# Memory values of a two-layer decoder step: the value slabs become the moving operand

## The reference

```python
def mem_kv(mem, w_kv):
    B, M, _ = mem.shape                     # 1, 256, 1024
    k, v = jnp.split(jnp.einsum('bmd,de->bme', mem, w_kv), 2, axis=-1)
    return k.reshape(B, M, M_HEADS, M_HD), v.reshape(B, M, M_HEADS, M_HD)
...
s = jnp.einsum('bthd,bmhd->bhtm', q, mk) * M_SCALE
o = jnp.einsum('bhtm,bmhd->bthd', softmax(s), mv)
```

## Time and profile before

| what | value |
|---|---|
| median of 3 runs | 2196.74 us (2196.38 to 2198.42) |
| profiled execution, its own time | 2196.69 us |
| its span, first to last instruction | 2194.9 us |
| PE busy in the span | 2154.5 us, 98% |
| PE weight loads | 1961.4 us, 89% |
| DVE, ACT, POOL busy | 77%, 60%, 46% |
| memory products, layer 0 and layer 1 | 69 to 161 us, 1156 to 1236 us |

### The profile page before, as it was taken

How to read it: one execution, slowest core, us unless ns; L and a number is a source line. 1 busy time by engine, 2 the same in 40 slices (tenths; PEclk the granted TensorE clock), 3 DMA queues, 4 the chain that set the end, 5 groups by cost and what they waited for, 6 DMA issues and landing times.

```text
span 2194.9 us, 45729 instructions
## 1 busy us (share of the span) xinstructions
PE 2154.5 (98%) x15517; PEld 1961.4 (89%) x15517; DVE 1686.1 (77%) x3908; ACT 1316.4 (60%) x3002; POOL 1014.2 (46%) x820
## 2 busy tenths in 40 slices
PE   8989999999999999999999999999999999999998
PEld 8879799999999877888888988999999998788887
DVE  7766489979999856666656656999799996566666
ACT  6544474557777555555566645645777765555555
POOL 6764447997777610000043344589877774000000
PEclk9999999999999999999999999999999999999999
DMA  7548554554444665555545584455444447555554
GB/s 263 161 143 326 206 179 156 171 176 156 155 159 156 206 218 182 193 194 194 193 164 180 191 362 136 166 168 171 167 155 160 156 147 246 195 192 193 194 195 135
DMA packets 112422, 409.32 MB, mean 186 GB/s; under 512 B 16553, under 2 KB 18769, under 8 KB 107089
## 3 DMA queue, kind: packets, MB, share of 16 engines
q1 hardware_dynamic: 107744, 391.45, 52.2%
q0 software_dynamic: 4528, 15.86, 2.3%
HBM read 397.11 MB, written 10.14 MB: 186 GB/s over the span
## 4 chain that ended last, share of the span: by engine, by line
PE 62%; DVE 16%; POOL 7%; issue 4%; ACT 2%; POOLq 0%; ACTq 0%; DVEq 0%
PE banks L2712 10%; PE banks L2714 10%; PE banks L2713 10%; POOL slab_ring_lo L2150 7%; DVE one_hot_gates L2458 7%; PE banks L2201 5%; PE banks L2202 5%; PE banks L2203 5%; PE banks L296 3%; PE banks L297 3%; PE banks L298 3%; DVE slab_ring_lo L272 2%; DVE expert_activations L2475 2%; PE banks L2223 1%; DVE expert_activations L2466 1%
## 5 line engine op out<-in xcount | busy, mean ns | idle before, releaser
L2150 POOL TENSOR_TENSOR slab_ring_lo<-slab_ring,u_hi 128x512 fp32r<-128x512 f32 x504 | 663.1, 1340 | 167.5 <-ACT u_hi L2255 166.7
L2201 PE MATMUL banks<-operand_hi,u_hi 128*128 128x264 f32 x2016 | 584.8, 290 | 1.6 <-POOL slab_ring_lo L2150 1.6
L2203 PE MATMUL banks<-operand_hi,slab_ring_lo 128*128 128x264 f32 x2048 | 583.3, 285 | 0.0
L2202 PE MATMUL banks<-operand_lo,u_hi 128*128 128x264 f32 x2016 | 573.5, 284 | 0.0
L272 POOL TENSOR_TENSOR slab_ring_lo<-slab_ring,slab_hi 128x512 fp32r<-128x512 f32 x162 | 216.5, 1341 | 593.7 <-ACT slab_hi L262 593.0
L2656 DVE TENSOR_TENSOR v_lo<-slab_ring,v_hi 128x512 fp32r<-128x512 f32 x508 | 350.0, 691 | 117.7 <-ACT v_hi L2616 113.0
L2712 PE MATMUL banks<-v_hi,w_hi 128*128 128x512 f32 x1000 | 391.1, 391 | 3.4 <-DVE w_lo L2652 2.2
L2714 PE MATMUL banks<-v_lo,w_hi 128*128 128x512 f32 x1000 | 389.2, 389 | 0.0
L2713 PE MATMUL banks<-v_hi,w_lo 128*128 128x512 f32 x1000 | 389.2, 389 | 0.0
L2255 ACT ACTIVATE u_hi<-slab_ring 128x512 fp32r<-128x512 f32 x504 | 317.7, 631 | 117.8 <-PE banks L2203 115.2
L2203 PEld LDWEIGHTS banks<-operand_hi,slab_ring_lo 128*128 128x128 f32 x2048 | 385.4, 188 | 0.0
(11 more groups left out here) (443 smaller groups left out, 3794.1 us busy)
## 6 DMA issues: line engine op xcount, KB each, us to landing
slab_ring<-in_u SPq DMA_DIRECT2D x256, 512.0 KB
slab_ring<-in_v SPq DMA_DIRECT2D x256, 512.0 KB
slab_ring<-in_proj SPq DMA_DIRECT2D x144, 512.0 KB
cache_k_T<-in_cache_k SPq DMA_DIRECT2D x16, 1024.0 KB, 8.7
cache_v<-in_cache_v SPq DMA_DIRECT2D x16, 1024.0 KB, 11.8
memory_T<-in_mem POOLq DMA_DIRECT2D x2, 1024.0 KB, 6.5
sample_state<-in_state POOLq DMA_DIRECT2D x8, 256.0 KB, 3.9
out_mem_k_out<-mem_k_T SPq DMA_DIRECT2D x16, 128.0 KB, 3.0
```

Source lines behind the costliest of these rows:

```text
L2150: nc.gpsimd.tensor_tensor(step.ring_lo[:, s, g * HC:(g + 1) * HC, :], step.slab(s)[:, g * HC:(g + 1) * HC, :], part[:, buf].bitcast(F32), ...
L2201: nc.tensor.matmul(bank, part[:, buf, k, :], xh[:, c, :], start=(c == 0), stop=False)
L2202: nc.tensor.matmul(bank, part[:, buf, k, :], xl[:, c, :], start=False, stop=False)
L2203: last = nc.tensor.matmul(bank, step.ring_lo[:, s, c, :], xh[:, c, :], start=False, stop=(c == DC - 1))
```

## The change

For the value slabs the roles are exchanged. The memory tokens become stationary, as two blocks of 128 tokens per chunk, and the slab's 128 columns move. The result comes out with tokens on the partitions, in two halves of 128 columns of one bank, so the two transposes, the copy to `memory_values_T`, that buffer and two semaphores go. A value slab has 8 chunks x 2 token blocks x 3 = 48 matmuls with 128 moving columns in place of 24 with 256, and one ScalarE copy in place of two, issued right behind the product. Keys are made as before.

```diff
     def product(self, pe, k):
         if k >= 2:
             pe.wait_ge(self.read, k - 1)
-        product(self.step, pe, self.base + k, self.bank_of + k % 2, None, self.mem, NMEM)
-
-    def transpose(self, pe, k):
         if k < DC:
-            return
-        nc = self.step.nc
-        pe.wait_ge(self.copied, k - DC + 1)
-        for m in range(NMEM // P):
-            last = nc.tensor.transpose(self.bank(k)[:, NMEM + m * P:NMEM + (m + 1) * P],
-                                       self.values_T[:, k % 2, m * P:(m + 1) * P], self.step.ident)
-        last.then_inc(self.turned, 1)
+            product(self.step, pe, self.base + k, self.bank_of + k % 2, None, self.mem, NMEM)
+        else:
+            self.values(pe, k)
+
+    def values(self, pe, k):
+        step, nc, n = self.step, self.step.nc, self.base + k
+        j = step.split_number[n]
+        xh, xl = self.mem
+        wh, wl = step.slab_hi[:, (j + 1) % 2], step.ring_lo[:, n % SLOTS]
+        for c in range(DC):
+            if c % HC == 0:
+                pe.wait_ge(step.slab_lo_ready[c // HC], j + 1)
+            for m in range(NMEM // P):
+                out, ts = self.bank(k)[:, m * P:(m + 1) * P], slice(m * P, (m + 1) * P)
+                nc.tensor.matmul(out, xh[:, c, ts], wh[:, c, :], start=(c == 0 and m == 0), stop=False)
+                nc.tensor.matmul(out, xl[:, c, ts], wh[:, c, :], start=False, stop=False)
+                last = nc.tensor.matmul(out, xh[:, c, ts], wl[:, c, :], start=False,
+                                        stop=(c == DC - 1 and m == NMEM // P - 1))
+            if c == HC - 1:
+                last.then_inc(step.half_product_done, 1)
+        last.then_inc(step.product_done, 1)
 
     def copy(self, act, k):
         step, nc = self.step, self.step.nc
         act.wait_ge(step.product_done, step.product_count(self.base + k))
-        if k < DC:
-            nc.scalar.activation(step.mem_k[:, k, :], self.bank(k)[:, 0:NMEM], ACT.Copy).then_inc(self.read, 1)
-        else:
-            nc.scalar.activation(self.values_T[:, k % 2, :], self.bank(k)[:, 0:NMEM], ACT.Copy).then_inc(self.copied, 1)
-
-    def copy_transposed(self, act, k):
-        if k < DC:
-            return
-        step, nc = self.step, self.step.nc
-        act.wait_ge(self.turned, k - DC + 1)
-        out = step.mem_v[:, :, (k - DC) * P:(k - DC + 1) * P]
-        nc.scalar.activation(out, self.bank(k)[:, NMEM:2 * NMEM].rearrange("p (m f) -> p m f", m=NMEM // P),
-                             ACT.Copy).then_inc(self.read, 1)
+        out, bank = step.mem_k[:, k % DC, :], self.bank(k)[:, 0:NMEM]
+        if k >= DC:
+            out = step.mem_v[:, :, (k - DC) * P:(k - DC + 1) * P]
+            bank = bank.rearrange("p (m f) -> p m f", m=NMEM // P)
+        nc.scalar.activation(out, bank, ACT.Copy).then_inc(self.read, 1)
...
                 def memory_pair(k):
                     memory.product(pe, k)
-                    memory.transpose(pe, k - 1)
...
                     memory.copy(act, k)
-                    memory.copy_transposed(act, k - 1)
```

More of the change, by code:

```diff
@@ L898, in __init__ @@
         self.step, self.base, self.mem, self.bank_of = step, base, mem, bank
-        self.values_T = None
         self.read = step.sem(f"memory_chunk_copied{layer}")
-        self.copied = step.sem(f"memory_value_chunk_copied{layer}")
-        self.turned = step.sem(f"memory_value_chunk_transposed{layer}")
     def bank(self, k):
@@ L969, in hgrn_pool_mixer @@
         mem_hi = sb("memory_hi", [P, DC, NMEM], ctx, F32R)
-        values_T = sb("memory_values_T", [P, 2, NMEM])
         rows = sb("sample_value_key_rows", [NS, 2, P])
@@ L1024, in hgrn_pool_mixer @@
         memory = MemoryProducts(step, layer, base + 20, (mem_hi, mem_lo), 4)
-        memory.values_T = values_T
         with ExitStack() as c1, nc.Block("mixer_in", no_gpsimd_drain=True) as block:
@@ L1430, in _ @@
                 memory_pair(15)
-                memory.transpose(pe, 2 * DC - 1)
             @block.scalar
@@ L1486, in _ @@
                 high_and_copy(15)
-                memory.copy_transposed(act, 2 * DC - 1)
             @block.gpsimd
@@ L1752, in window_mixer @@
             memory = MemoryProducts(step, layer, base, (mem_hi, mem_lo), 6)
-            memory.values_T = sb("memory_values_T1", [P, 2, NMEM], c1)
             QK = ((0, P), (P, 3 * P))
@@ L1870, in _ @@
                     memory.product(pe, h)
-                    if h:
-                        memory.transpose(pe, h - 1)
                     if h + 2 < HEADS_C:
@@ L2007, in _ @@
                     memory.copy(act, h)
-                    if h:
-                        memory.copy_transposed(act, h - 1)
                     if h == HEADS_C - 2:
```

## The result

The changed kernel takes 2232.47 us (median of 5, 2231.1 to 2232.98), the kernel before 2198.42 us (5 runs beside it, 2196.38 to 2199.59): ratio 1.0159, 95% interval 1.0146 to 1.0171. It is 34.05 us slower. The forecast was +34.0 us, 2230.7, from the 2196.74 known then.

What follows compares the result with a forecast made beforehand. PE was taken to pace the value slabs; 40.3 (products) - 1.7 (transposes) - 3.6 (waits) - 1.0 (ends) = +34.0 us on the median of 2196.74, giving 2230.7 us, range 2223 to 2241.

Steps and rivals of the forecast that it cites:

- The product: Each value product: 48 matmuls 0.111 us apart, set by the weight load; 5.33 us against 2.81, +40.3 us over 16 slabs.
- The transposes and waits: Transposes gone at eight full places, -1.7 us; PE's waits before products 13 to 15 of layer 0 gone, -3.6 us.
- The ends: Ends of the value stretches: -0.2 us in layer 0, -0.5 and -0.3 in layer 1, together -1.0 us.
- The clock: Rival: value slabs at 1.2 GHz, 2314 us if all, chance 0.03; margin behind layer 0: up to 1.7 us either way.
- clock full: Expected profile sign: the granted clock stays full with the new value products.
- a clock at half in these stretches: Sign that would prove the prediction wrong: half clock in the value slabs' stretches.
- Hidden loads: Rival: fp32r loads go in under the short stream, distance 0.057 to 0.062 us, 2190.1 to 2193.8 us; chance 0.04.
- the distance of 0.081: Rival: value matmuls near 0.081 us apart, a product 3.92 us, sum +11 us, 2208 us; chance 0.03.
- float32's price: Rival: narrow fp32r value matmuls cost as much as plain float32, 10.7 us a product, +120, 2317 us; chance 0.06.

Runs made afterwards that it cites:

- filler: Idle transposes of a constant put where PE was idle; in the changed kernel, behind layer 0's product 15 and at the next part's start: 2231.95 us.

## Why the prediction was right

**The product.** 5.33 us forecast, 5.28 measured; 2.47 more for a slab in place of 2.52, so 39.5 and not 40.3 us. That the load sets the distance was argued and is now shown, by halving it, and by doubling the stream for 6% of the product's time. By the Trainium skill (TensorE: Matmul & The Clock Gate, "Back-to-back issue gap") a stream of load and matmul pairs takes about 81 ns each at 128 columns, and the estimate from that figure was +11 us. The trace has 111 ns for fp32r loads of 128 columns, and the measurement decides.

**The transposes and waits.** Taken together 6.3 us forecast; the kernel without them is 6.5 us faster, 7.1 by its trace. In layer 1 I had 1.7 to 2.1 us and the stretch shows 16 x 2.47/2 - 17.7 = 2.1. No new wait took their place.

**The ends.** That POOL's last half would hold layer 0's end was right. From the last product's end to the next part it is 3.79 us now (175.59 to 179.38) and was 4.03 (160.90 to 164.93): 0.24 gained, 0.2 forecast.

**The clock.** It was priced as a rival and as a margin of 1.7 us either way, and the profile was to show "clock full". It did move, +1.5 us net. By the prediction's own sign, a clock at half in these stretches, that part of it was wrong: 3.41 us of layer 0's value stretch ran at 1.2 GHz, between two value products though, not in one. The terms without the clock are 39.5 - 7.1 = 32.4 us, and the two stretches without their 1.6 at 140.57 are 32.5; with the clock the terms give 33.9. So the mechanism held, and that the sum hit 34.0 to the tenth is luck: the products were put 0.8 us too dear and the savings 0.8 too small, and these 1.6 stood in for the clock, which the sum had at nothing.

**The rivals.** Hidden loads, the distance of 0.081 and float32's price did not come. The clock's fall inside value products came only with 64 moving columns.

What stays open: why the clock falls near 141 us. All three traced kernels with 128 stationary and 128 moving columns in layer 0 have it (140.57, 142.49, 142.97), and none of the eight others does (the one with 64 moving columns, whose clock falls in many places, aside), among them the one that streams 256 columns with the same loads and the one with half loads. One profile each; that thin streaming makes it is likely and not shown apart from what follows it there, which is PE's work on the sampled tokens and a wait of 0.8 us; that work and that wait are in the kernels without the fall too. It is also open why the fall behind layer 0 lasts 6.83 us in the changed kernel and in the one changed in layer 0 alone, and 3.41 in the six others without filler.

## What to carry to other kernels

In these traces a matmul costs the larger of its weight load and its stream. With fp32r, 128 stationary columns take 0.111 us to load and 256 moving ones 0.118 to stream, so 128 moving columns cost nearly what 256 do: before you exchange the roles, count the loads, not the multiplications, and keep 256 columns on the moving side, under which the load is hidden. A short transpose on PE (0.11 us) can be much cheaper than a product that avoids it, if it is issued where its inputs are ready and its result isn't awaited. Where PE idles, as for 2.3 us behind layer 0 in the kernel before, look at the granted clock behind it as well as at the wait.

## What the runs showed of the hardware that was not expected

The clock fell to 1.2 GHz while PE loaded weights without a pause: 64 moving columns per load of 128, 0.11 us apart, held 2.4 GHz for some 5 us of the first product and then not. With 128 moving columns it held through 16 us of back-to-back products (159.5 to 175.6). The weight load slows with the clock, 0.213 us for 128 columns against 0.111, so such a product costs nearly double. Half a load (64 columns) is fully hidden under 128 moving columns, at 0.06 us each.
